# Part of the gates' work moved into the recurrence's last chunk, and the head means taken off by a constant

## The reference, cut to what matters

```python
def step(state, inp):
    r_t, w_t, k_t, v_t, kk_t, a_t = inp
    sa = jnp.einsum("bhvk,bhk->bhv", state, kk_t)
    state = (state * w_t[:, :, None, :]
             - sa[..., None] * (kk_t * a_t)[:, :, None, :]
             + v_t[..., None] * k_t[:, :, None, :])
    return state, jnp.einsum("bhvk,bhk->bhv", state, r_t)
...
_, out = lax.scan(step, state0, xs)
out = jnp.moveaxis(out, 0, 1)
mean = jnp.mean(out, axis=-1, keepdims=True)
var = jnp.mean(jnp.square(out - mean), axis=-1, keepdims=True)
out = ((out - mean) * lax.rsqrt(var + GN_EPS)).reshape(b, s, w_) * lnx_w + lnx_b
bonus = (jnp.sum(rh * kh * r_k, axis=-1, keepdims=True) * vh).reshape(b, s, w_)
return (out + bonus) * g, v_first
...
gates = jax.nn.sigmoid(proj[..., OFF_GATE:OFF_RWKV].reshape(b, s, N_BRANCH, D_MODEL) + gate_b)
branches = jnp.einsum("bsnc,ncd->bsnd", ys, branch_proj)
merged = jnp.einsum("bsnd,bsnd->bsd", gates, branches)
```

## Time and profile before

| What | Value |
|---|---|
| Time, median of 3 runs | 2055.4 us (2055.26 to 2056.12) |
| The profiled execution's own time | 2059.97 us |
| Its span, first to last instruction | 2058.2 us |
| TensorE busy | 2003.2 us, 97% of the span |
| VectorE, ScalarE, GpSimd busy | 1068.8, 796.4, 136.1 us (52, 39, 7%) |
| Mean granted TensorE clock | 0.985 |
| Last chunk from its products n = 2 to the stage's last instruction | 384.05 to 414.25 us |
| Gate stage, first output tile | 414.56 to 456.73 us |

### The profile page before, as it was taken

The page is one execution under the profiler, slowest core; times in us unless marked ns, Lnnn a source line. Parts: engine busy times, 40 slices in busy tenths (PEclk is TensorE's granted clock), DMA queues, the critical chain, the costliest instruction groups (busy, mean ns, idle before and its releaser), DMA issues. The chain is left out here.

```text
span 2058.2 us, 29318 instructions
## 1 busy us (share of the span) xinstructions
PE 2003.2 (97%) x11736; PEld 1611.1 (78%) x11736; DVE 1068.8 (52%) x1763; ACT 796.4 (39%) x1281; POOL 136.1 (7%) x167
## 2 busy tenths in 40 slices
PE   8999999999999999999999999998999999999997
PEld 6677768868888878888888767886777788888886
DVE  5665775374445535477765344228554653423433
ACT  5433532243234424444443222225666543313321
POOL 0000345400000000000000000000101000000000
PEclk9999999989999999999999999999999999999998
DMA  4232220032332430233223414222111222233232
GB/s 175 72 113 93 69 80 3 3 108 92 97 97 93 153 110 14 92 98 96 95 99 115 157 64 134 93 92 63 42 52 42 82 93 91 92 100 95 96 98 82
DMA packets 48417, 181.95 MB, mean 88 GB/s; under 512 B 5456, under 2 KB 5968, under 8 KB 47664
## 3 DMA queue, kind: packets, MB, share of 16 engines
q1 hardware_dynamic: 44384, 166.66, 25.1%
q0 software_dynamic: 2768, 11.85, 1.7%
q10 hardware_dynamic: 1152, 1.89, 0.3%
HBM read 176.13 MB, written 4.24 MB: 88 GB/s over the span
## 5 line engine op out<-in xcount | busy, mean ns | idle before, releaser
L209 DVE TENSOR_TENSOR weights_lo<-weights_raw,weights_hi 128x1024 fp32r<-128x1024 f32 (+2 forms) x288 | 365.5, 1269 | 785.2 <-ACT weights_hi L201 784.7
L201 ACT ACTIVATE weights_hi<-weights_raw 128x1024 fp32r<-128x1024 f32 (+2 forms) x288 | 314.1, 1091 | 813.3 <-PE sp_ps L234 251.1
L232 PE MATMUL sp_ps<-arena_parts,weights_hi 128*128 128x512 f32 x720 | 283.4, 394 | 3.0 <-DVE arena_parts L303 2.5
L234 PE MATMUL sp_ps<-arena_parts,weights_lo 128*128 128x512 f32 x720 | 281.0, 390 | 0.0
L233 PE MATMUL sp_ps<-arena_parts,weights_hi 128*128 128x512 f32 x720 | 280.7, 390 | 0.0
L232 PE MATMUL end_ps<-arena_parts,weights_hi 128*128 128x512 f32 x576 | 225.9, 392 | 0.5 <-DVE arena_parts L305 0.5
L233 PE MATMUL end_ps<-arena_parts,weights_hi 128*128 128x512 f32 x576 | 225.3, 391 | 0.0
L234 PE MATMUL end_ps<-arena_parts,weights_lo 128*128 128x512 f32 x576 | 225.1, 391 | 0.0
L232 PE MATMUL fr_ps<-arena_parts,weights_hi 128*128 128x512 f32 (+1 forms) x480 | 182.3, 380 | 1.9 <-DVE arena_parts L305 1.1
L233 PE MATMUL fr_ps<-arena_parts,weights_hi 128*128 128x512 f32 (+1 forms) x480 | 180.6, 376 | 0.0
L234 PE MATMUL fr_ps<-arena_parts,weights_lo 128*128 128x512 f32 (+1 forms) x480 | 180.5, 376 | 0.0
(11 more groups left out here) (391 smaller groups left out, 3009.7 us busy)
## 6 DMA issues: line engine op xcount, KB each, us to landing
weights_raw<-w_up SPq DMA_DIRECT2D x44, 512.0 KB, 3.4
weights_raw<-w_proj SPq DMA_DIRECT2D x38, 512.0 KB, 3.4
weights_raw<-w_gates SPq DMA_DIRECT2D x32, 576.0 KB, 3.7
weights_raw<-w_ca SPq DMA_DIRECT2D x32, 512.0 KB, 3.4
weights_raw<-w_down SPq DMA_DIRECT2D x16, 704.0 KB, 4.1
weights_raw<-w_in SPq DMA_DIRECT2D x22, 512.0 KB, 3.5
weights_raw<-w_logits SPq DMA_DIRECT2D x16, 512.0 KB, 3.5
weights_raw<-w_ff1a SPq DMA_DIRECT2D x16, 512.0 KB, 3.4
```

The source lines that it names most:

```text
L201: act.activation(self.w_hi[:, g % 2, 0:cols], self.raw[:, g % 2, 0:cols], ACT.Copy).then_inc(self.hi_ready, 1)
L209: dve.tensor_tensor(self.w_lo[:, g % 2, 0:cols], self.raw[:, g % 2, 0:cols], self.w_hi[:, g % 2, 0:cols].bitcast(F32), ALU.subtract).then_ ...
L232: pe.matmul(out, left[0], right[0], start=start, stop=False)
L234: return pe.matmul(out, left[1], right[0], start=False, stop=stop)
```

## The change

1. A new constant `centre`, the identity less 1/64 within each head's block, takes the place of the identity when the values are turned (u < 4), as a plain float32 matmul in place of a transpose. The values by token then have mean zero over each head, and so have the recurrence's outputs; `means` and `centre` of `TimeMixOut` go, with their semaphores. The mask constant is half as long.
2. The gates' input is split, and the eight gate products of the first output tile's first gate (m = 0 to 7) are done, inside the last chunk (`GateLead`): product 0 between products and step 2, product 1 after solve_lower, 2 between products and step 4, 3 after step 4, 4 to 7 after solve_upper, carry_down, solve_lower and finish. Low part k is queued on VectorE after update k + 1 for k < 4, the rest in the tail; the first two branch tiles are split in the tail as well. `right_side` of the last chunk moves from behind step 5 to before products(3, 5).
3. In the gate stage the first output tile goes in the order 8, 9, 12, 13, variances, 14, 15, 16, 10, 11, 17 to 20, spread_out, 21 to 35. VectorE's and ScalarE's orders change with it. The PSUM tensor is held across the two stages.

```diff
 CONSTS = [
-    ("zeros", 384), ("ident", 128), ("ones", 128), ("head_ones", 128), ("upper", 128), ("causal4", 512), ("neg_tri", 128),
+    ("zeros", 384), ("ident", 128), ("ones", 128), ("head_ones", 128), ("upper", 128), ("causal2", 256), ("centre", 128), ("neg_tri", 128),
     ("level", 768), ("flip", 128),
...
         for c in range(NW):
-            mm = pe.transpose(self.ps[:, n, c * P:(c + 1) * P], source[:, c, n * P:(n + 1) * P], self.core.c("ident"))
+            to, block = self.ps[:, n, c * P:(c + 1) * P], source[:, c, n * P:(n + 1) * P]
+            if u < 4:
+                mm = pe.matmul(to, block, self.core.c("centre"), start=True, stop=True)
+            else:
+                mm = pe.transpose(to, block, self.core.c("ident"))
         mm.then_inc(self.turned, 1)
...
+    core.held = ExitStack()
-        whole = ctx.enter_context(nc.psum_tensor("proj_ps", [P, 8, T], F32))
+        whole = core.front_ps = core.held.enter_context(nc.psum_tensor("front_ps", [P, 8, T], F32))
-        chunks = time_mix_chunks(core, whole, breaks, lace, g0 + 39)
+        chunks = time_mix_chunks(core, whole, breaks, lace, g0 + 39, GateLead(core, whole, g0 + 38))
...
-def time_mix_chunks(core, ps, breaks, lace, gates):
+def time_mix_chunks(core, ps, breaks, lace, gates, lead):
...
     LEVELS, HALF = 6, 4 * HD
+    LEAD_AT = [(1, 2), (1, 3), (0, 0), (0, 1)]
     GRAM, INVERSE, X, O, Z = 0, 2, 4, 6, 7
...
             for c, side, h in both:
-                pe.matmul(o_ps(c, side), v_tok[:, ch, head_cols(h)], gram(ch, h)[:, 384:512], start=(ch == 0 and c == 0), stop=False,
-                          skip_group_check=True)
+                mm = pe.matmul(o_ps(c, side), v_tok[:, ch, head_cols(h)], gram(ch, h)[:, 384:512], start=(ch == 0 and c == 0), stop=False,
+                               skip_group_check=True)
+            if ch == NT - 1:
+                mm.then_inc(lead.room, 1)
         def solve_upper(ch):
...
                 gram_unit(0, kind, c)
+        def between(ch, kind, c):
+            if ch < NT:
+                gram_unit(ch, kind, c)
+            elif (kind, c) in LEAD_AT:
+                lead.product(pe, LEAD_AT.index((kind, c)))
+            if (ch, kind, c) == (NT, 0, 1):
+                right_side(NT - 1)
         for ch in range(NT):
...
             products(ch, 1)
-            gram_unit(ch + 1, 1, 0)
+            between(ch + 1, 1, 0)
             step(ch, 1)
             carry_down(ch - 1)
-            gram_unit(ch + 1, 1, 1)
+            between(ch + 1, 1, 1)
             products(ch, 2)
-            gram_unit(ch + 1, 1, 2)
+            between(ch + 1, 1, 2)
             step(ch, 2)
             solve_lower(ch - 1)
-            gram_unit(ch + 1, 1, 3)
+            between(ch + 1, 1, 3)
             products(ch, 3)
...
             products(ch, 4)
-            gram_unit(ch + 1, 0, 0)
+            between(ch + 1, 0, 0)
             step(ch, 4)
-            gram_unit(ch + 1, 0, 1)
+            between(ch + 1, 0, 1)
             products(ch, 5)
-            gram_unit(ch + 1, 0, 2)
+            between(ch + 1, 0, 2)
             step(ch, 5)
-            gram_unit(ch + 1, 0, 3)
-        right_side(NT - 1)
+            between(ch + 1, 0, 3)
         solve_upper(NT - 1)
+        lead.product(pe, 4)
         carry_down(NT - 1)
+        lead.product(pe, 5)
         solve_lower(NT - 1)
+        lead.product(pe, 6)
         finish(NT - 1)
+        lead.product(pe, 7)
     def gpsimd(pool):
...
                .then_inc(out_ready, 1)
+        def ahead(ch, *tiles):
+            if ch == NT - 1:
+                for k in tiles:
+                    lead.split.hi(act, k)
         for ch in range(NT):
...
             take_products(ch, 1)
+            if ch == NT - 1:
+                act.wait_ge(x_back, 16)
+            ahead(ch, 0)
             take_rest(ch - 1)
             take_products(ch, 2)
+            ahead(ch, 1, 2)
             take_products(ch, 3)
+            ahead(ch, 3)
             take_out(ch - 1)
             take_products(ch, 4)
+            if ch == NT - 1:
+                ahead(ch, 4)
+                take_upper(ch)
             take_products(ch, 5)
-        take_upper(NT - 1)
+            ahead(ch, 5, 6)
         take_rest(NT - 1)
+        ahead(NT - 1, 7)
+        for k in range(2):
+            lead.y_split.hi(act, k)
         take_out(NT - 1)
...
-                              core.c("causal4", 2 * P * kind, 2 * P).unsqueeze(1).broadcast_to([P, 2, 2 * P]), ALU.mult)\
+                              core.c("causal2").unsqueeze(1).broadcast_to([P, 2, 2 * P]), ALU.mult)\
...
         dve.wait_ge(unit_ready, 1)
+        def ahead(ch, *tiles):
+            if ch == NT - 1:
+                for k in tiles:
+                    lead.split.lo(dve, k)
         for ch in range(NT):
...
             update(ch, 1)
+            ahead(ch, 0)
             mask(ch + 1, 1, 1)
...
             update(ch, 2)
+            ahead(ch, 1)
             negate(ch - 1, sa_done, slice(HD, P), sa_ready)
...
             next_state(ch - 1)
+            ahead(ch, 2)
             mask(ch + 1, 0, 0)
...
             update(ch, 4)
+            ahead(ch, 3)
             mask(ch + 1, 0, 1)
...
             mask(ch + 1, 0, 3)
+        dve.wait_ge(lead.room, 1)
+        ahead(NT - 1, 4)
         negate(NT - 1, upper_done, slice(0, HD), upper_ready)
+        ahead(NT - 1, 5, 6)
         negate(NT - 1, sa_done, slice(HD, P), sa_ready)
+        ahead(NT - 1, 7)
+        for k in range(2):
+            lead.y_split.lo(dve, k)
     return sync, tensor, gpsimd, scalar, vector
...
     return halves(32), halves(36)
+def gate_input(core, k):
+    return core.pair(34, 42 if k < 4 else 46, k)
+class GateLead:
+    BANK = 1
+    def __init__(self, core, ps, group):
+        self.core, self.ps, self.group = core, ps, group
+        self.split = h_split(core, "gt_x", "norm_mix", lambda k: gate_input(core, k))
+        self.room = core.sem("gl_room")
+        self.y_split = core.branch_split = Split(core, "gt_y", lambda k: core.arena[:, k, :], lambda k: core.pair(12, 20, k))
+        del core.stage_sems[-2:]
+    def product(self, pe, k):
+        if k == 0:
+            self.core.wait_weights(pe, self.group)
+        pe.wait_ge(self.split.lowered, k + 1)
+        product(pe, self.ps[:, self.BANK, :], self.core.weights(self.group, k * P, (k + 1) * P), gate_input(self.core, k), k == 0, k == KD - 1)
 class TimeMixOut:
...
         self.spread, self.spread_in = head_spread(core), core.sem("to_spread_in")
         self.inverted, self.rstd_spread = core.sem("to_inverted"), core.sem("to_rstd_spread")
         self.squared, self.var_done = core.sem("to_squared"), core.sem("to_var_done")
...
         sp.wait_ge(self.spread_in, 16)
-    def means(self, pe):
-        for c in range(NW):
-            pe.matmul(self.ps[:, self.mean_banks[c], :], self.core.c("head_ones"), self.out[:, c, :], start=True, stop=True)\
-              .then_inc(self.mean_done, 1)
     def variances(self, pe):
-        pe.wait_ge(self.centred, 1)
         for c in range(NW):
...
         pe.wait_ge(self.inverted, 1)
-        pe.wait_ge(self.centred, NW)
         for c in range(NW):
...
     def take_square(self, act, c):
-        act.wait_ge(self.centred, c + 1)
         act.activation(self.square[:, c, :], self.out[:, c, :], ACT.Square).then_inc(self.squared, 1)
...
         act.activation(self.rstd, self.rstd, ACT.Sqrt).then_inc(self.rooted, 1)
-    def centre(self, dve, c):
-        dve.wait_ge(self.mean_done, c + 1)
-        dve.scalar_tensor_tensor(self.out[:, c, :], self.ps[:, self.mean_banks[c], :], -1.0 / HD, self.out[:, c, :], ALU.mult, ALU.add)\
-           .then_inc(self.centred, 1)
     def shift(self, dve, c):
...
         self.scale_at = a[:, MIX_SCALE, :]
-        self.x_split = h_split(core, "gt_x", "norm_mix", self.x)
-        self.y_split = Split(core, "gt_y", lambda k: a[:, k, :], lambda k: core.pair(12, 20, k))
+        self.y_split = core.branch_split
         self.r_split = Split(core, "gt_r", lambda k: a[:, 8 + k, :], lambda k: core.pair(30, 46, k))
...
         self.g0, _ = core.plan(32, 0)
-    def x(self, k):
-        return self.core.pair(34, 42 if k < 4 else 46, k)
     def branch(self, k):
...
                 core.wait_weights(pe, g, 0 if d is None else d - 1)
-            if d is None and n == 0 and k < KD:
-                pe.wait_ge(self.x_split.lowered, k + 1)
-            elif d is None and k >= KD and n < 2:
+            if d is None and k >= KD and n < 2:
                 pe.wait_ge(self.y_split.lowered, 4 * n + k - KD + 1)
...
             if k < KD:
-                mm = product(pe, self.ps[:, 2 + 2 * n, :], w, self.x(k), k == 0, k == KD - 1)
+                mm = product(pe, self.ps[:, 2 + 2 * n, :], w, gate_input(core, k), k == 0, k == KD - 1)
             else:
...
                 mm.then_inc(core.groups_done, 1)
-        to.means(pe)
-        to.variances(pe)
-        for m in range(36):
-            if m == 10:
```

(53 more changed lines are left out.)

## The result

Changed kernel: median 2058.6 us over 19 runs (2055.03 to 2063.19); kernel before, run on the same chips, 2055.68 us over 19 (2053.98 to 2058.24). Ratio 1.0017, 95% interval 1.0011 to 1.0023, so +3.5 us, +2.3 to +4.7 (the two medians lie 2.9 us apart). The predicted 2057.4 is +2.0 on the median before: right in sign and kind (no change within 0.2%), 1.5 us short against the before of the same batch. How much of that is luck is told further down.

What follows compares the result with a forecast made beforehand. TensorE (PE), busy 97% of the span, was taken to bound the kernel. Turns +2.3, recurrence +3.7, gate stage -8.1 and clock +4.1 gave +2.0 us, median 2057.4 us, range 2051.9 to 2062.0 with 2 in 10 outside.

Steps and rivals of the forecast that it cites:

- The turns: Turning of the values: sixteen transposes become float32 products at 0.24 us in place of 0.10, +2.3 us, bounds +1.6 and +5.8.
- rival B: Turns: load and columns of the constant's product do not overlap, 0.46 us each, +5.8 in place of +2.3; chance 0.05.
- The recurrence: Last chunk: eight gate products add 5.5 us of PE, new waits replace old ones; +3.7 us at full clock.
- a gate product (three matmuls) costs 0.69 us: Price of each product moved into the recurrence's last chunk; eight make +5.5 us of PE.
- rival A: Recurrence: the clock falls there too, right_side and tail at half, +1.7 to +3.4 us; chance 0.18.
- the 2.0 us that the half clock cost in the tail before: Recurrence's tail: L1338 and L1353 ran at half clock before; full clock after the change was assumed, within the +3.7.
- The gate stage: First gate matmul to second output tile's first product: 34.1 us at full clock against 42.2, -8.1 us; VectorE sets it.
- The wait before m = 18: Gate stage: PE waits 3.4 us, until S+13.7 (S the stage's first matmul), for weight group 2's low part.
- The second: Gate stage: PE waits 4.4 us before m = 27 for weight group 3's low part, ready at S+27.9.
- The clock in the gate stage: A fall to half clock behind each of the two long waits, 1.9 + 2.2 = +4.1 us, bounds +1.7 and +6.0.
- Sum: Whole kernel: +2.3 + 3.7 - 8.1 + 4.1 = +2.0 us, median 2057.4 us.
- What set the stage: Gate stage after the change: VectorE's queue sets it, and PE's freed time is spent waiting for it.

Runs made afterwards that it cites:

- x3: Changed kernel with lead products 1, 2 and 3 put later, where their low parts are ready; 2053.2 us, 0.9993 of the kernel before.
- x8: The changed kernel once more, unedited; 2058.09 us, 1.001 of the kernel before.
- x2: Changed kernel with the values turned by plain transposes again, so the mean is not taken off at all; 2055.1 us, 1.0 of the kernel before.
- x6: Changed kernel with 13 idle matmuls before m = 18 and 17 before m = 27, results unread; 2058.11 us, 1.002 of the kernel before.
- x4: Changed kernel with weight group 2 split before ScalarE's root and right behind VectorE's variance; 2058.11 us, 1.0006 of the kernel before.
- x5: x3 with VectorE's and ScalarE's gate-stage queues reordered to the order PE wants; 2049.65 us, 0.997 of the kernel before.
- x7: x2 with the means and their subtraction back at the head of the gate stage; 2057.63 us, 1.0008 of the kernel before.

## Why it came out so

- **The turns**, predicted +2.3 us (0.24 us each): +1.83, 0.213 us each. L1303's row was the right neighbour; rival B is out. The Trainium skill ("TensorE: Matmul & The Clock Gate", Terms) calls the transpose mode four times faster for FP32; this trace has 1.71 us for eight products against 0.79 for eight transposes, 2.2 times.
- **The recurrence**, predicted +3.7 us with no fall of the clock: +5.1. The mechanism was right, and the waits stood where they were put, none longer than forecast (predicted 0.5, 0.5, 1.4, 1.1; measured 0.47, 0.20, 1.19, 0.95). The mis-sized term is "a gate product (three matmuls) costs 0.69 us", read from thirteen in a row. Among narrow products it costs 0.89: its first matmul takes 0.34 us to the next one's start and its last 0.33, where those in a row take 0.23. Eight times 0.2 is 1.6 us, against a miss of 1.4. x3 shows the waits to be removable (-3.0 us in the profile).
- **The clock in the recurrence** (rival A, given 0.18): it fell there in three profiles of six, for 4.2 to 4.5 us, above the +1.7 to +3.4 of its price. This chance is the step that was worst. Nor did it fall where the rival had it, at product 3's wait with right_side behind it, but behind the wait before solve_upper. The text said that five busy microseconds between two waits spoke against it; PE was busy for those (403 to 411 in x8), and the clock fell all the same after the next wait. The forecast also credits the change with the 2.0 us that the half clock cost in the tail before, which holds only where it doesn't fall.
- **The gate stage**, predicted 34.1 us at full clock and about 38.2 with the clock's loss: 37.65, 34.48 (x2) and 36.25 (x8). The wait before m = 18 was forecast as 3.4 us and ended at S+13.7; it is 2.94 us and ends at S+13.78. Up to there the chain of VectorE was counted to a tenth (the terms as written add up 0.1 us short of some of their sums: 412.6 + 5.5 + 0.1 is 418.2, 6.3 + 1.1 + 1.6 is 9.0; nothing hangs on it). The second, forecast as 4.4 us, is 2.65 us in x3, about 1.0 in x2 and x8, and missing in the change's own profile, where PE at 1.2 GHz was the later one.
- **The clock in the gate stage**, predicted +4.1 us for two falls: one fall, of 17 us. It made the first spread 1.0 us longer and the three products before it 2.1 us, so that finishes and group 3 came 3.1 us later than forecast (S+31.0 for S+27.9), and PE came 0.5 us later still: 3.6 us. Half the clock for 17 us is 8.5 us' worth, five times the 1.7 that was counted for one stretch; 3.6 of it was on the path. In the other two profiles with this order the stage is 0.4 us (x2) and 2.2 us (x8) above the 34.1 at full clock. So +4.1 was twice the mean of the three, and that it fits the first is chance. That a filled wait keeps the clock is seen in x6, without a gain in time.
- **Sum.** In the change's first profile +2.4 us, in x8's (+1.8, 40.43 - 31.16 = +9.3, 36.25 - 42.17 = -5.9) +5.2; the mean, +3.8, is within the timed +2.3 to +4.7, but both are set against a single profile of before. The forecast of +2.0 is near because its errors cancel: in that mean the recurrence has 3.5 us more than forecast (rival A's share and the products), the gate stage 1.2 less and the turns 0.5 less. In time, the runs' mean clock puts up to about 2 of the +3.5 us on the clock (0.9858 against 0.9868; an estimate, with the clock of before from the experiments' batches).
- **What set the stage.** The prediction held that VectorE's queue sets it. x4 and x5 show it: with PE's instructions of the gate stage unchanged, the order of VectorE's and ScalarE's queues takes E - S from 36.11 (x3) to 29.64 (x5), 6.5 us, what the clock gives back with the waits gone included. Timed, x5 is 4.7 us below x3 by the ratios (0.997 against 0.9993, in two batches). The change left a queue that was laid out around eight input products that PE no longer had to do there.

**Open:** why x6 gains nothing in time; why the clock falls in the recurrence in one execution and not in the next of the same program. The change's profile also has 0.5 us more than that of before between 303 and 309 us, where nothing differs: PE pauses there among sixteen L1275 matmuls, idle for 0.23 us before 305.12, and the profile names nothing that it waited for. The profiles of x2 and x7 have such a pause at the same place (0.46 and 1.51 us idle), the other seven have none; its cause is open too. Whether the lead is worth its price in x5's order, as against the constant alone in such an order, wasn't tried.

## What to carry to other kernels

Work that is moved into a wait pays only where its operands are ready before that wait; otherwise it brings a wait of its own, and everything on its queue stands behind it. When work leaves a stage, lay out anew the queue of the engine that comes next (here weight splits ahead of the reciprocal and between the finishes): that took 6.5 us off the stage in the profiles and 4.7 us off the time here; leaving out the means took 3.5 us off the stage in the profiles. One profile of such a kernel is no measure of what the clock costs it: look at the clock of all runs. Price an inserted product between the neighbours that it will have, start to start, not from a run of its own kind.

## What the runs showed of the hardware

- A 128x512 product of three matmuls costs 0.68 us among its like and 0.89 to 0.91 us among 64x64 float32 products.
- A float32 product with a 128x128 block and 128 columns leaves two records and costs 0.213 us (1.71 for eight), a transpose of the same size 0.10 (0.79 for eight, x2).
- The same instructions ran in 36.24 us and in 40.43 us in two profiles of one program, by the granted clock alone.
- In the change's first profile the clock stayed at 1.2 GHz from 433 to 450 us, with PE busy for 16 of these 17 us, 7.19 of them in the spreads (matmuls of 8 rows), which take 3.69 us in x5; in x2, behind the same wait, it was at full clock up to 439.
- Executions of one program (x2) took 2051.20 to 2061.03 us, with mean granted clocks of 0.990 to 0.985.
